# Layer-norm sums, the last layer's weight places and a page load's place in the queue, in a two-layer decoder step

## The reference, cut to what matters

```python
def trunk(x, ...):
    for layer in range(2):
        if layer == 0:
            h, state = mlstm_mixer(x, w_in, b_gate, w_out, C0, n0, m0)   # chunkwise matrix memory
        else:
            kv = x @ w_kv                                   # shared K and V
            q = x @ w_q
            h = attend(q, ctx) @ w_out_b                    # samples: paged cache, 64 pages of K and of V
        x = layer_norm(ALPHA * x + h, ln_g[layer, 0], ln_b[layer, 0])
        x = layer_norm(ALPHA * x + square(relu(x @ w_up[layer])) @ w_down[layer], ln_g[layer, 1], ln_b[layer, 1])

def layer_norm(x, g, b):                # over the 1024 values of a token
    mu = x.mean(-1); var = square(x - mu).mean(-1)
    return (x - mu) * rsqrt(var + 1e-5) * g + b
```

## Time and profile before

| | |
|---|---|
| median of three runs | 923.85 us |
| the profiled execution's own time | 924.06 us |
| its span, first to last instruction | 922.3 us |
| granted clock of TensorE, mean | 0.997 of full |
| PE busy | 911.1 us, 99% |
| PE's share of the chain of work that ended last | 98% |
| PEld, DVE, ACT, POOL busy | 92%, 68%, 47%, 6% |
| DMA, mean over the span | 198 GB/s |

### The profile page before, as it was taken

How to read it: one execution, slowest core, us unless ns; L and a number is a source line. 1 busy time by engine, 2 the same in 40 slices (tenths; PEclk the granted TensorE clock), 3 DMA queues, 4 the chain that set the end, 5 groups by cost and what they waited for, 6 DMA issues and landing times.

```text
span 922.3 us, 18832 instructions
## 1 busy us (share of the span) xinstructions
PE 911.1 (99%) x7545; PEld 847.8 (92%) x7545; DVE 625.0 (68%) x1095; ACT 435.3 (47%) x819; POOL 53.8 (6%) x67
## 2 busy tenths in 40 slices
PE   9999999999999999999999999999999999999996
PEld 8999888899999999999888778978999999999975
DVE  6577567778977575677576847456568797657526
ACT  5445556466445263445344453344447635536320
POOL 0000002500000000230000000000230000000000
PEclk9999999999999999999999999999999999999999
DMA  9973214654445544466898997998945455544301
GB/s 285 265 227 105 93 47 108 211 168 155 143 142 154 166 138 141 164 236 214 313 306 287 353 367 269 400 400 352 284 139 181 139 174 181 149 137 143 133 1 57
DMA packets 131147, 182.77 MB, mean 198 GB/s; under 512 B 5843, under 2 KB 112027, under 8 KB 131060
## 3 DMA queue, kind: packets, MB, share of 16 engines
q1 hardware_dynamic: 125754, 177.54, 58.3%
q10 hardware_dynamic: 4666, 1.92, 0.8%
q0 software_dynamic: 640, 2.10, 0.6%
HBM read 175.22 MB, written 6.32 MB: 197 GB/s over the span
## 4 chain that ended last, share of the span: by engine, by line
PE 98%; DVE 1%; DMA 1%; ACT 0%; issue 0%; DVEq 0%; ACTq 0%
PE ps L611 24%; PE ps L613 23%; PE ps L612 23%; PE ps L976 6%; PE ps L1018 3%; PE ps L1074 3%; PE ps L864 1%; PE ps L866 1%; PE ps L865 1%; PE ps L854 1%; PE ps L625 1%; DMA x_tok<-in_x_sample_dram 1%; PE ps L729 0%; PE ps L873 0%; PE ps L796 0%; PE ps L949 0%
## 5 line engine op out<-in xcount | busy, mean ns | idle before, releaser
L1176 ACT ACTIVATE w_hi<-raw 128x1024 fp32r<-128x1024 f32 x192 | 202.4, 1057 | 241.5 <-PE ps L613 221.1
L1559 DVE TENSOR_TENSOR w_lo<-raw,w_hi 128x1024 fp32r<-128x1024 f32 x192 | 236.5, 1234 | 112.0 <-ACT w_hi L1176 111.6
L611 PE MATMUL ps<-x_hi,w_hi 128*128 128x322 f32 (+1 forms) x888 | 279.5, 315 | 0.0
L613 PE MATMUL ps<-x_hi,w_lo 128*128 128x322 f32 (+1 forms) x888 | 276.3, 311 | 0.0
L612 PE MATMUL ps<-x_lo,w_hi 128*128 128x322 f32 (+1 forms) x888 | 275.8, 311 | 0.0
L611 PE MATMUL ps<-h_hi,w_hi 128*128 128x320 f32 x568 | 176.2, 310 | 0.5 <-DVE h_lo L1697 0.5
L613 PE MATMUL ps<-h_hi,w_lo 128*128 128x320 f32 x568 | 175.3, 309 | 0.0
L612 PE MATMUL ps<-h_lo,w_hi 128*128 128x320 f32 x568 | 175.2, 309 | 0.0
L611 PEld LDWEIGHTS ps<-x_hi,w_hi 128*128 128x128 f32 x888 | 168.0, 189 | 5.2 <-ACT k_turned L1459 2.9
L612 PEld LDWEIGHTS ps<-x_lo,w_hi 128*128 128x128 f32 x888 | 168.5, 190 | 0.2
L613 PEld LDWEIGHTS ps<-x_hi,w_lo 128*128 128x128 f32 x888 | 167.4, 189 | 0.0
(11 more groups left out here) (342 smaller groups left out, 975.0 us busy)
## 6 DMA issues: line engine op xcount, KB each, us to landing
raw<-in_w_up_dram SPq DMA_DIRECT2D x32, 1024.0 KB, 5.7
raw<-in_w_down_dram SPq DMA_DIRECT2D x32, 1024.0 KB, 5.4
page<-in_cache_k_dram SPq DMA_DIRECT2D x64, 512.0 KB, 5.5
page<-in_cache_v_dram SPq DMA_DIRECT2D x64, 512.0 KB, 8.9
raw<-in_w_in_a_dram SPq DMA_DIRECT2D x12, 1024.0 KB, 9.7
raw<-in_w_kv_dram SPq DMA_DIRECT2D x8, 1024.0 KB, 7.4
raw<-in_w_out_a_dram SPq DMA_DIRECT2D x4, 1024.0 KB, 5.5
raw<-in_w_q_b_dram SPq DMA_DIRECT2D x4, 1024.0 KB, 5.2
```

The lines of the kernel that those rows point to most:

```text
L611: mm(out, WH[PLACE[t]][:, k, :], hi[:, k, 0:width], start=(k == 0), stop=False)
L613: last = mm(out, WL[PLACE[t]][:, k, :], hi[:, k, 0:width], start=False, stop=(k == 7))
L1176: A(WH[PLACE[t]][:, :, :], raw_tile(t), ACT.Copy)\
L1559: V.tensor_tensor(WL[PLACE[t]][:, :, :], raw_tile(t), WH[PLACE[t]][:, :, :].bitcast(F32), ALU.subtract)\
```

## The change

Four parts of the program are altered.

1. The layer norms' sums: POOL adds six pairs instead of seven; PE adds the eighth chunk itself (`X[:, 7]` and its square in `FS[1]`), with two more matmuls by ones, and all four stand at the end of the first tile instead of in the middle of the second.
2. The last quad's weight places: the fifth place is gone and the tiles rotate through four; four values of k are done at once and four are left for later (48 matmuls instead of 60).
3. The sample's last steps: the multiplication by rsqrt goes from DVE to ACT and the addition of the bias to POOL; DVE does them no more, and takes `y_stats` of prompt block 0 first.
4. SP's order: the wait for 16 scored pairs and the load of V page NPG + 3 stand ahead of K page 37 instead of K page 44; unit 4 * Q_WV + 2 keeps its place after page 41.

The counts of the semaphores `s_st` and `s_yf` follow. The lines that begin with # name the engine and are no part of the program.

```diff
-PLACE[8 * Q_LAST + 4:] = [4, 0, 1, 2]

-        WH.append(put("w_hi4", [128, 8, 128], F32R, yt_at))
-        WL.append(put("w_lo4", [128, 8, 128], F32R, yt_at))

 # SP
             load_unit(4 * Q_WV + 1)
-            pages(34, 42)
-            load_unit(4 * Q_WV + 2)
-            pages(42, 44)
+            pages(34, 37)
             sp.wait_ge(s_sc, 16)
             load_page(NPG + 3)
-            pages(44, NPG)
+            pages(37, 42)
+            load_unit(4 * Q_WV + 2)
+            pages(42, NPG)
...
+            sp.wait_ge(s_yad, 1)
+            sp.dma_start(y_sample.rearrange("b t c -> (b t) c"), Yt[0:64, 2, :]).then_inc(s_yp, 16)
             sp.wait_ge(s_yf, 1)
-            sp.dma_start(y_sample.rearrange("b t c -> (b t) c"), Yt[0:64, 2, :]).then_inc(s_yp, 16)
-            sp.wait_ge(s_yf, 2)
             sp.dma_start(y_prompt[0, 0:128, :], Yt[:, 0, :]).then_inc(s_yp, 16)
             for i in range(2):
-                sp.wait_ge(s_yf, i + 3)
+                sp.wait_ge(s_yf, i + 2)

 # PE, at the end of first_dense
                 dense(t, XH, XL, lambda k: (s_xl, (8, 16, 24)[l] + k + 1), TW)
+                ln_stats(l)

-            def ln_stats(l, t):
-
-                def ready(k):
-                    if k == 3:
-                        pe.wait_ge(s_st, 7 * l + 7)
-                        mm(ps[2][:, 0:T], ones, A1[:, :], start=True, stop=True).then_inc(s_lnp, 1)
-                        mm(ps[3][:, 0:T], ones, A2[:, :], start=True, stop=True).then_inc(s_lnp, 1)
-                    return s_lo, t + 1
-                return ready
+            def ln_stats(l):
+
+                pe.wait_ge(s_st, 6 * l + 6)
+                mm(ps[2][:, 0:T], ones, A1[:, :], start=True, stop=False)
+                mm(ps[3][:, 0:T], ones, A2[:, :], start=True, stop=False)
+                pe.wait_ge(s_xr, 8 * l + 8)
+                mm(ps[2][:, 0:T], ones, X[:, 7, :], start=False, stop=True).then_inc(s_lnp, 1)
+                pe.wait_ge(s_sqd, 8 * l + 8)
+                mm(ps[3][:, 0:T], ones, FS[1][:, :], start=False, stop=True).then_inc(s_lnp, 1)

 # PE, last_down
-                for k in range(3):
+                for k in range(4):
                     pe.wait_ge(s_lo, t + k + 1)
...
                     down_sample(k).then_inc(s_mm, 1)
-                    for n in ((0, 1, 2), (3, 4), (5, 6))[k]:
+                    for n in ((), (0, 1, 2), (3, 4), (5, 6))[k]:
                         x_turn(n)
-                for k in range(3, 8):
-                    if k == 7:
-                        x_turn(7)
+                for k in (4, 5, 6):
                     pe.wait_ge(s_lo, t + k + 1)
-                    last = down_sample(k)
-                last.then_inc(s_acc, 1)
+                    down_sample(k)
+                x_turn(7)
+                pe.wait_ge(s_lo, t + 8)
+                down_sample(7).then_inc(s_acc, 1)
                 for i in range(2):
                     for half in range(2):
-                        for k in range(3, 8):
+                        for k in (4, 5, 6, 7):
                             last = down_prompt(k, i, half)
                         last.then_inc(s_acc, 1)

 # PE, two callers (the layers' second up tile, and the second tile of w_q)
-                            dense(t, XH, XL, ln_stats(l, t) if i == 0 and n == 1 else None, TW)
+                            dense(t, XH, XL, None, TW)

 # ACT
-                elif t >= SPL:
-                    act.wait_ge(s_mm, 8 * Q_MLP1 + 48)
...
                 A(rsc[0:w, i:i + 1], rsc[0:w, i:i + 1], ACT.Exp, scale=-0.5).then_inc(s_rs, 1)
+                if i == 2:
+                    act.wait_ge(s_yg, 1)
+                    A(Yt[0:64, 2, :], Yt[0:64, 2, :], ACT.Copy, scale=rsc[0:64, 2:3]).then_inc(s_ysc, 1)

 # DVE, after y_var(2)
-            dve.wait_ge(s_gbr, 32)
-            ins = y_gained(2, slice(0, DM), Yt[0:64, 2, :])
-            own(ins)
-            y_refined(2)
-            y_final(2, slice(0, DM))
             dve.wait_ge(s_acc, 2)
             y_stats(0, 0, summed(0, 0))
+            y_refined(2)
+            dve.wait_ge(s_gbr, 32)
+            y_gained(2, slice(0, DM), Yt[0:64, 2, :]).then_inc(s_yg, 1)
             dve.wait_ge(s_acc, 3)

 # POOL (the same for layer norms 0 and 1)
-            for n in range(1, 8):
+            for n in range(1, 7):
                 sums(2, n)
+            pool.wait_ge(s_ysc, 1)
+            G.tensor_tensor(Yt[0:64, 2, :], Yt[0:64, 2, :], gbR[0:64, 1, :], ALU.add).then_inc(s_yad, 1)
```

More of the change, by code:

```diff
@@ L354, in build @@
         s_evr, s_evt, s_gbr = sem("eps_row_done"), sem("eps_turned"), sem("gain_bias_rows_in")
-        s_acc, s_yl = sem("y_tokens_summed"), sem("y_sample_low")
+        s_acc, s_yl, s_yg, s_ysc, s_yad = [
+            sem(n) for n in ("y_tokens_summed", "y_sample_low", "y_sample_gained", "y_sample_scaled", "y_sample_biased")]
         s_aol = sem("attn_out_lo")
@@ L927, in _ @@
             for n in range(1, 8):
-                dense(8 * Q_WQ + n, XH, XL, ln_stats(1, 8 * Q_WQ + 1) if n == 1 else None, TW)
+                dense(8 * Q_WQ + n, XH, XL, None, TW)
             def p_scores(h):
@@ L1320, in squared @@
                 if n >= 2:
-                    act.wait_ge(s_st, 7 * l + max(n - 2, 1))
+                    act.wait_ge(s_st, 6 * l + max(n - 2, 1))
                 A(FS[n % 2][:, :], X[:, n, :], ACT.Square).then_inc(s_sqd, 1)
@@ L1832, in y_final @@
             def y_final(i, c):
-                w = 64 if i == 2 else 128
-                V.scalar_tensor_tensor(Yt[0:w, i, c], Yt[0:w, i, c], rsc[0:w, i:i + 1], gbR[0:w, 1, c], ALU.mult, ALU.add)\
+                V.scalar_tensor_tensor(Yt[:, i, c], Yt[:, i, c], rsc[:, i:i + 1], gbR[:, 1, c], ALU.mult, ALU.add)\
                     .then_inc(s_yf, 1)
@@ L2164, in sums @@
                 if not first:
-                    pool.wait_ge(s_st, 7 * l + n - 1)
+                    pool.wait_ge(s_st, 6 * l + n - 1)
                 G.tensor_tensor(A1[:, :], X[:, 0, :] if first else A1[:, :], X[:, n, :], ALU.add)
```

## The result

The changed kernel took 929.86 us (median of four runs, 928.38 to 933.16), the kernel before 923.95 beside it. The ratio is 1.0076, with a 95% interval of 1.0052 to 1.0099: slower by 7.0 us (4.8 to 9.1), where the forecast was 4.5. Seven executions of the changed kernel lie between 928.4 and 933.2. The profiled one took 931.34 us with a span of 929.5, 7.2 more than before; all that follows is read from it.

A forecast was written before the change was run, and what follows sets the result against it. PE was taken to bound the kernel, with 98% of the chain. Sums 3.1, places 0, tail 1.2 and pages 0.2 gave 4.5 us on the profiled 924.06: 928.6, so 928.4 for the median, range 926.7 to 930.6.

The forecast's parts named there:

- PE sets the time, so an added matmul costs its interval: Layer norms' sums: added matmuls by ones cost 0.54 us each, 3.2 us, less 0.13 us of waiting in layer 0: net 3.1.
- The new waits of the statistics are covered: Layer norms: everything the four matmuls read is ready 1.7 us ahead, so PE doesn't wait.
- Places: 0, and the split of tile 7 is covered: Last product: PE's total is unchanged and its other matmuls cover the last tile's split; 0, at most 2.4 us.
- Tail, 1.2 us: Samples' last steps: POOL's 2.6 us addition holds DVE's y_refined and y_final until +10.0; DVE comes 1.2 us late, bounds 0 to 2.5.
- Page order, 0.2 us: SP's queue: page 42 lands at 522.1, PE turns it at 523.59; some 1 us of cover, 0.2 us charged, bounds 0 and 3.7.
- late page: SP's queue: K pages run dry at page 42 or 43, 1 to 3.7 us on top, about 930.5; chance 11%.

The follow-up runs named there:

- E3: The kernel before with only the layer norms' sums changed (PE adds the eighth chunk): ratio 1.0035, +3.2 us.
- E8: The kernel before with the statistics' two matmuls at k = 5 instead of k = 3 of the second tile: ratio 0.9997.
- E4: The kernel before with only the four weight places; DVE finishes the samples as before: ratio 1.0016, +1.5 us.
- E7: The kernel before with the four weight places and the samples' last steps on ACT and POOL: ratio 1.0005, +0.5 us.
- E6: The kernel before with only the samples' last steps moved to ACT and POOL, five places kept: ratio 0.9992.
- E11: The kernel before with the wait ahead of K page 37, but V page NPG + 3 loaded behind K page 47: ratio 1.0011, +1.0 us.
- E1: The kernel before with only the page order changed (wait and V page NPG + 3 ahead of K page 37): ratio 1.0032, +3.0 us.

## Why the prediction was wrong

The direction held, and the pages ran short at the very page that I had worked out; the sizes of the terms didn't hold, and that of the page order decides. 4.5 us were forecast with a range to 930.6. The median of the changed kernel's four runs, 929.86, lies in it; the ratio against the runs beside it puts it at 931.0 (928.8 to 933.1), above it and 2.5 us above the forecast.

1. *PE sets the time, so an added matmul costs its interval.* Right: 0.54 us each (E3, and the chain after). Net 2.9 in E3's trace instead of 3.1, since the 0.68 of L835 in layers 1 and 2, which I read as the break between kinds of matmul, was a wait for POOL as well (E8), and the 0.13 of layer 0 was 0.27. The three waits are 0.56 in all, by which the part should cost 2.7; the last 0.2 stays open. I had POOL's row of 403.17 and used it only for the collision on DVE.
2. *The new waits of the statistics are covered.* Right: no wait for x, the squares or POOL.
3. *Places: 0, and the split of tile 7 is covered.* PE never waited for a split, right. That the part is worth 0 for PE and takes 2.8 us from DVE's cover was in the text, but it was charged to POOL's addition alone. E4 shows that the places cost 1 us by themselves. Places and tail together were put at 1.2 and came to 0.8 (E7), so the 0 here was partly made good by a tail that was put too high, which is luck.
4. *Tail, 1.2 us.* The mechanism was right in each step: y_refined held until POOL was through at +9.8 (forecast +10.0), y_stats with no idle time ahead of it. It came to 0.7 to 0.8. The addition took 2.39 us and not 2.6, and only one of y_refined's three instructions is lengthened, so y_final follows 0.44 after POOL and not 0.6. The port lock that the Trainium skill states (SBUF — State Buffer, "SBUF: two separate sides") agrees with E6 and with the changed kernel: the blocked instruction ends with POOL's. The Trainium skill's 4497 ns for 2048 columns (GPSIMD Engine Reference, "Performance versus the Vector engine") gives an estimate of 2.3 us, nearer to the 2.39 than my rows did.
5. *Page order, 0.2 us.* This is the step that failed. I had the whole chain: wait at 507.5, V page, five pages, unit, page 42, and a cover of about 1 us. The issues came at the forecast pace (some 2 us later, as PE was), and the V page landed at 513.9, 3.6 us after its issue (forecast 3.4). Two terms were wrong. The first is the supply, taken as 1.30 us for each load, one behind the other, from the 402 GB/s of a running stream. From the V page's landing to page 42's, at 527.1, the eight page-sized loads took 13.2 us instead of 10.4. That makes 2.8 us more, against a cover of 1.5 at page 42, and the wait was 1.6. The windows and the queue of SP, changed kernel (that of SP from 509.5 to 527.1 us: packets, MB, share):

```profile
513.90:527.10 13.20, 11.70 (x157) 8.62 (x155) 11.76 (x22) 5.55 (x11) 0.00 (x0) 1.00 1.03 374
...
q1 hardware_dynamic: 2240, 5.45, 87.6%
```

   The transfers were not slow: 374 GB/s is 7% under 402, which is 0.9 us of the 2.8. The other 1.9 are data that the forecast didn't place ahead of page 42. At 374 GB/s 4.94 MB were moved in the 13.2 us, and eight loads hold 4.19. The stores of K rows are 0.16 of the difference (the forecast had 0.4 us for them, off its cover). The rest belongs to pages issued behind page 42: since 509.5 the queue had moved 5.45 MB, while everything up to page 42 is 4.72, so 0.73 MB of later pages were in before page 42 was complete. The landings keep their order all the same. The table under E11 says the same in another way: 1.30 us for each load, and some 3 us once. That those 3 us are there after every such pause is not shown.

   The other term was missing: I priced a stall at its own length, and behind it PE ran at the lower clock for another 1.75 us. With both, the part costs 3.5 us in this trace, and 2.3 in E1's, where the clock stayed up; why it did there is open. The Trainium skill describes this for waits longer than these (TensorE: Matmul & The Clock Gate, "HAM oscillation — how this bites in real kernels"): a wait for a transfer lets the clock fall, and the next work starts cold. Three traces agree in part (0.76, 0.75 and 0.66 in the worst window): the clock fell, but only over a microsecond after the work had begun again. E1's, with a wait as long, doesn't agree.

The rival "late page" had the right mechanism and the right place, page 42, with a chance of 11%, and its time, 930.5, was nearest to the 931.0. That its time fits is in part luck: it named the wait alone, and half of what the pages cost here came from the clock.

No version here beats the kernel before beyond doubt. E8's edit is the only one that takes something off PE, 0.56 us by the chain, and by its runs it can't be told from the kernel before.

## What to carry to other kernels

When a wait is moved forward in a queue that feeds a busy engine, count the data that must pass between the end of the wait and the first late consumer, and allow for what is issued behind it too: here 0.73 MB of later loads were moved before the awaited one was complete, and the loads took 3 us more than their sizes at full rate. A cover of 1.5 us was too little for that. Price a stall of the matrix engine above its length, for the clock behind it may be lower. Where two parts of a change share a cover (PE's remaining matmuls and DVE's chain in the tail), work out each part alone too, or a cost is charged to the wrong one.

## What else the runs showed of the hardware

A short wait for several semaphores can be missing from the list of waits and still be in the chain: 0.14 us for POOL three times, seen only because one and the same pair of passes was 0.68 long in one place and 0.54 in another.

The clock at the start is not the same in each execution. The same work, 40 to 50 us after the start, in the kernel before and in E6, which are the same program there:

```profile
40.00:50.00 10.00, 10.00 (x69) 9.66 (x69) 4.74 (x14) 2.54 (x4) 2.29 (x8) 0.83 0.89 275
```

```profile
40.00:50.00 10.00, 10.00 (x79) 9.66 (x79) 4.51 (x14) 2.88 (x4) 2.20 (x8) 1.00 0.88 260
```

A clock of 0.83 over 10 us is 1.7 us of work at full rate. E6's and E8's profiled spans, 921.2 and 920.7 us, are short for that reason, which is why the parts were weighed by stretches from the first cut on, and not by spans.
